# One of four channel blocks of the wide convolution moved to GpSimd

## What is computed

```
def conformer_conv(h_val, h_gate, dw_w, dw_b, ln_g, ln_b):
    h = h_val * jax.nn.sigmoid(h_gate)
    h = causal_depthwise_conv(h, dw_w) + dw_b        # 31 taps, 512 channels
    h = layer_norm(h, ln_g, ln_b)
    return jax.nn.silu(h)

def hybrid_mixer(x, w_in, ...):
    h = x @ w_in
    c_val, c_gate, q, k, v, z, b_logit, a_logit = jnp.split(h, IN_SPLITS_2, axis=-1)
    y_conv = conformer_conv(c_val, c_gate, ...)
    y_dn = gated_deltanet(q, k, v, z, b_logit, a_logit, ...)
    return jnp.concatenate([y_conv, y_dn], axis=-1) @ w_out
```

## Time and profile before

| | |
|---|---|
| median of the three runs | 2535.86 us |
| the profiled execution | 2543.58 us |
| its span | 2541.5 us |
| TensorE busy | 96% of the span |
| VectorE busy | 74% |
| ScalarE busy | 56% |
| GpSimd busy | 0.2 us |
| mixer A, from the first projection to the last output product | about 995 to 1177 us |
| mixer B | about 1375 to 1561 us |

### The profile page before, as it was taken

The page is one execution under the profiler, slowest core; times in us unless marked ns, Lnnn a source line. Parts: engine busy times, 40 slices in busy tenths (PEclk is TensorE's granted clock), DMA queues, the critical chain, the costliest instruction groups (busy, mean ns, idle before and its releaser), DMA issues.

```text
span 2541.5 us, 36256 instructions
## 1 busy us (share of the span) xinstructions
PE 2433.5 (96%) x14462; PEld 2103.4 (83%) x14462; DVE 1880.7 (74%) x2198; ACT 1424.2 (56%) x1578; POOL 0.2 (0%) x4
## 2 busy tenths in 40 slices
PE   7999999999999999989999998999999999999897
PEld 7999989899998998886997885787777777888786
DVE  7665755567657543986554985889999999988787
ACT  4654444456545343423342422678888888777574
POOL 0000000000000000000000000000000000000000
PEclk9999999999999999999999998999999999999998
DMA  6333464343345444304534302899999999999796
GB/s 253 138 119 133 154 244 183 149 146 145 117 162 203 178 188 165 134 36 166 199 150 155 145 3 100 337 360 404 412 412 413 413 413 412 382 347 367 287 354 261
DMA packets 119623, 593.19 MB, mean 233 GB/s; under 512 B 17440, under 2 KB 17824, under 8 KB 77472
## 3 DMA queue, kind: packets, MB, share of 16 engines
q1 hardware_dynamic: 110224, 585.40, 59.8%
q10 hardware_dynamic: 9232, 5.47, 0.8%
HBM read 589.79 MB, written 1.05 MB: 232 GB/s over the span
## 4 chain that ended last, share of the span: by engine, by line
PE 69%; DVE 18%; DMA 5%; issue 4%; ACT 3%; DVEq 0%; SPq 0%; ACTq 0%; POOLq 0%
PE bank L608 21%; PE bank L2512 17%; PE bank L865 12%; DVE wlo L687 6%; DMA ring<-in_stream 5%; PE bank L1717 4%; DVE ring_lo L839 2%; ACT whi L682 2%; PE bank L1133 2%; DVE big L2967 1%; PE bank L1148 1%; PE bank L1738 1%; PE bank L1903 1%; PE bank L2452 1%; DVE big L2141 1%
## 5 line engine op out<-in xcount | busy, mean ns | idle before, releaser
L687 DVE TENSOR_TENSOR wlo<-ring,whi 128x2048 fp32r<-128x2048 f32 x430 | 979.0, 2289 | 113.0 <-ACT whi L682 108.8
L682 ACT ACTIVATE whi<-ring 128x2048 fp32r<-128x2048 f32 x433 | 825.9, 1912 | 111.6 <-PE bank L2512 51.4
L2512 PE MATMUL bank<-whi,xhi 128*128 128x512 f32 x896 | 367.7, 410 | 16.3 <-DVE wlo L687 12.5
L2512 PE MATMUL bank<-wlo,xhi 128*128 128x512 f32 x896 | 353.0, 394 | 0.0
L839 DVE TENSOR_TENSOR ring_lo<-ring,slot_hi 128x1024 fp32r<-128x1024 f32 x160 | 192.5, 1222 | 136.2 <-ACT slot_hi L816 125.9
L608 PE MATMUL bank<-xhi,whi 128*128 128x256 f32 x864 | 244.5, 283 | 2.4 <-DVE xlo L570 1.3
L608 PE MATMUL bank<-xhi,wlo 128*128 128x256 f32 x864 | 244.5, 283 | 0.0
L608 PE MATMUL bank<-xlo,whi 128*128 128x256 f32 x864 | 244.5, 283 | 0.0
L816 ACT ACTIVATE slot_hi<-ring 128x1024 fp32r<-128x1024 f32 x160 | 166.5, 1052 | 109.1 <-PE bank L865 79.1
L2512 PEld LDWEIGHTS bank<-whi,xhi 128*128 128x128 f32 x896 | 170.0, 190 | 64.8 <-DVE wlo L687 31.5
L865 PE MATMUL bank<-xh,slot_hi 128*128 128x256 f32 x704 | 203.1, 288 | 3.0 <-DVE ring_lo L839 3.0
(11 more groups left out here) (525 smaller groups left out, 4508.7 us busy)
## 6 DMA issues: line engine op xcount, KB each, us to landing
ring<-in_stream SPq DMA_DIRECT2D x555, 1024.0 KB, 7.2
par<-in_par ACTq DMA_DIRECT2D x2, 2048.0 KB, 9.1
con<-in_con SPq DMA_DIRECT2D x1, 1216.0 KB, 10.8
X<-in_x SPq DMA_DIRECT2D x2, 512.0 KB, 4.1
out_y<-X SPq DMA_DIRECT2D x2, 512.0 KB, 2.6
par<-in_par ACTq DMA_DIRECT2D x2, 448.0 KB, 6.0
par<-in_par ACTq DMA_DIRECT2D x2, 157.5 KB, 3.3
con<-in_con SPq DMA_DIRECT2D x1, 64.0 KB, 4.3
```

The lines of the kernel that those rows point to most:

```text
L682: act.activation(whi[:, k % NSPLIT, :], src, ACT.Copy).then_inc(act_done, AC.step(tag + f".w{k}"))
L687: v.tensor_tensor(wlo[:, k % NSPLIT, :], src, whi[:, k % NSPLIT, :].bitcast(F32), ALU.subtract)\
L2512: mm = pe.matmul(out, left, right, start=start and i == 0, stop=stop and i == len(pairs) - 1)
```

## The change

GpSimd computes block 3 in each mixer. It waits for `gated1`, makes the first tap with the bias, and then for each of 30 taps one multiplication into a product tile, `scr[:, 1, 768:1024]`, and one addition into `ca`. A semaphore of its own, `pool_taps`, goes up with each of these 61 instructions, and each waits for the one before. VectorE's steps of pair 1 make block 2 alone. Three waits for the 61st are added: TensorE's before the sum over the channels, VectorE's before the copy of N2 (whose neighbour N2 + I takes the tile of the products) and VectorE's before the centring.

```diff
+        pool_taps = sem("pool_taps")
...
                 if lev == 1:
                     pe.wait_ge(vec_done, VE.at(tag + "cc"))
+                    pe.wait_ge(pool_taps, 2 * CONV_WIN - 1)
                     pe.wait_ge(vec_done, VE.at(tag + "vb"))
                     over_channels(PS[6], lambda b: ca[:, b, :], "cmu")
...
             for t in range(NT):
                 v.wait_ge(pe_done, PE.at(tag + f"N2{t}"))
+                v.wait_ge(pool_taps, 2 * CONV_WIN - 1)
                 v.tensor_copy(mN2[t], PS[3 * t + 2][:, :]).then_inc(vec_done, VE.step())
...
                 if lev == 1:
+                    v.wait_ge(pool_taps, 2 * CONV_WIN - 1)
                     v.wait_ge(pe_done, PE.at(tag + "cmu"))
...
             for w in range(first, last):
-                for b in (2 * pair, 2 * pair + 1):
+                for b in (0, 1, 2)[2 * pair:2 * pair + 2]:
                     tap = dw[:, b * CONV_WIN + w:b * CONV_WIN + w + 1]
...
         @block.gpsimd
         def _(pool):
+            def last_block(tag):
+                b, product = 3, scr[:, 1, 768:1024]
+                pool.wait_ge(vec_done, VE.at(tag + "gated1"))
+                for w in range(CONV_WIN):
+                    src, at = cv[:, b, w:w + T], b * CONV_WIN + w
+                    if w == 0:
+                        pool.tensor_scalar(ca[:, b, :], src, p2("dww")[:, at:at + 1], p2("dwb")[:, b:b + 1], ALU.mult,
+                                           ALU.add).then_inc(pool_taps, 1)
+                        continue
+                    pool.wait_ge(pool_taps, 2 * w - 1)
+                    pool.tensor_scalar(product, src, p2("dww")[:, at:at + 1], None, ALU.mult).then_inc(pool_taps, 1)
+                    pool.wait_ge(pool_taps, 2 * w)
+                    pool.tensor_tensor(ca[:, b, :], ca[:, b, :], product, ALU.add).then_inc(pool_taps, 1)
+
             def body(tag):
                 def f(it):
-
+                    if tag in ("mixA", "mixB"):
+                        last_block(tag[3:])
                     pool.wait_ge(arrived, it * 4 + 4 * (seg_no[tag] + 1))
                     pool.sem_inc(pool_turns, 1)
-                    for s in (pe_done, act_done, vec_done, slots_used, slots_split):
+                    for s in (pe_done, act_done, vec_done, slots_used, slots_split, pool_taps):
                         pool.sem_clear(s)
```

## The result

The changed kernel takes 2550.33 us (median of 7 runs) where the kernel before takes 2535.95 (7 runs): 14.4 us more, a ratio of 1.0052 with a 95% interval of 1.0042 to 1.0063. It is slower, as forecast, by 14.4 us where 30.5 were forecast. The traces are of one execution each, and that of the kernel before took 2543.58 us: most executions of that kernel lie at 2532 to 2538 us, some (on two of the chips about half) at 2539 to 2544. In a second measurement, on the chip of the last experiment, the ratio was 1.0056 (1.0041 to 1.0070).

A forecast was written before the change was run, and what follows sets the result against it. TensorE, 96% busy, was taken to bound the kernel, with VectorE's work counting only where TensorE waits for it. Contention gave +13.8 in A, +15.0 in B and +1.7 for the clock: +30.5 on 2535.86, so 2566.4 us, range 2526 to 2594.

The forecast's parts named there:

- Rival 1: GpSimd's work costs VectorE nothing in either mixer: gain 7.3 us, 2528.6 us; chance 0.28.
- rival 2: GpSimd's block ends late and stalls VectorE's copy of N2 in each mixer: +28 us, 2564; chance 0.07.
- Two of the signs: GpSimd's 61 instructions from 1028.4 end near 1078; TensorE idles over 10 us before its norm sums in both mixers.
- 25.0 lost: VectorE, second gating to norm sums: each GpSimd instruction takes its whole time from a two-operand instruction, 61 x 0.41 us a mixer.
- the stretch: Stretch (a), second gating's end to end of projection 7's short convolution, 34.5 us: all of the block's price falls there.
- Less the idle: VectorE's waits for ScalarE before the norm sums absorb lost time: 5.25 us in A, 3.61 in B.
- 1.1 saved: VectorE before the end of projection 7's short convolution: four of pair 1's steps become single, 1.1 us a mixer.
- the slack of 1.4: Mixer A, before the norm sums: ScalarE's square ends at 1064.34, TensorE takes it up at 1065.78, 1.44 us absorbed.
- Forecast: 17.2: Mixer A: TensorE's norm sums come 17.2 us later, after savings, idle and slack are taken off the 25.0.
- 18.9: Mixer B: 18.9 us later, as 25.0 less 1.1, 3.61 of idle and 1.44 of slack.
- The gains: Behind the norm sums, shorter TensorE waits from VectorE's earlier decay product and following steps: 3.4 us in A, 3.9 in B.
- the 1.7 that I took for both: TensorE's low clock after the long idle before the norm sums: 1.7 us taken of 3.2 for both mixers.

The follow-up runs named there:

- the last experiment: Kernel before with four of VectorE's steps made earlier and nothing on GpSimd: 2538.08 us, ratio 1.0000; the changed kernel was run again beside it.
- the block made twice: Changed kernel, but GpSimd's 61 instructions go into a tile nobody reads and VectorE makes all four blocks: 2575.12 us, 1.0144 of the kernel before.
- twelve taps: Changed kernel, but GpSimd makes only block 3's first 12 taps, VectorE the rest, with its steps regrouped: 2551.36 us, 1.0054 of the kernel before.
- two inputs: Changed kernel with GpSimd's 30 multiplications by a scalar replaced by multiplications of two tensors, giving other numbers: 2839 us, in brackets.
- Without the block: Changed kernel with only the first of GpSimd's 61 instructions, block 3's other 30 taps left out: 2533.18 us, 0.9987 of the kernel before.
- changed again: The changed kernel run once more, unaltered, on the chip of the run with another VectorE order: 2551.07 us, 1.0056 of the kernel before.
- order alone: Kernel before with four of VectorE's ten steps around the decay product made earlier, nothing on GpSimd: 2538.08 us, ratio 1.0000.
- half width: Changed kernel with GpSimd's 60 instructions behind the first on 128 columns in place of 256: 2536.00 us, 0.9993 of the kernel before.
- one-input: Changed kernel with GpSimd's 30 additions replaced by multiplications by a scalar, so all 61 read one tensor: 2538.51 us, 1.0007 of the kernel before.

## Why the prediction was right and wrong

**The sign and the mechanism were right, the size was not.** Rival 1 (no contention) is out by the taps of 0.94 and 0.69 us and by the block made twice; rival 2 (GpSimd late) by the 23 us between its end and the copy. The rule of the Trainium skill on the shared pair of ports ("SBUF — State Buffer", "Who interferes with whom") agrees in what it separates: a two-operand instruction is held by a GpSimd instruction that reads, and by none that only writes. By its rule that one engine has the pair "for the whole instruction" the cost would be up to 0.97 and 0.72 us here; 0.22 and 0.47 were measured, and the measurement decides. The addition that the prediction estimates at 0.56 us lasts 0.72. Two of the signs weren't met: GpSimd ends at 1084.22 and not near 1078, and TensorE idles 6.3 us ahead of the norm sums in both mixers and not over 10. The range's upper end holds a slip: half of 0.41 us again is 0.62 an instruction and gives 2591, not 2594.

**The term that was mis-sized is "25.0 lost".** It had 61 instructions at 0.41, each taking turns with one of VectorE's, all ahead of the norm sums. Each factor was off. An instruction takes 0.22 or 0.47 of VectorE, 0.345 as a mean. GpSimd's own are 0.97 and 0.75 us long and 0.94 apart, more than twice the row that I took, so VectorE runs three instructions for two of GpSimd's; taking turns one for one never came about. And so only 46 of the 61 (43 us by 0.94) fall into the stretch, and a part of these lies beside PSUM operands and idle, where they cost nothing: 13.2 us in place of 25.0. The rest falls beside the taps ahead of the reciprocal and the short convolution of projection 8, under TensorE's projections 9 and 10. I had priced GpSimd's pace only for the question of whether it is in time, not for where its price falls.

**"Less the idle" was wrong the other way**, and hides a part of the first error. I took in all of the idle (5.25 and 3.61 us). The changed kernel still idles 1.40, and the run with twelve taps the full 2.78. Mixer A: 13.2 held - 1.1 saved - 3.85 of idle taken in = 8.3, against 8.5 by which the short convolution of projection 7 ends later (43.1 and 34.6 us behind the gating's end); less the slack of 1.4 it is the 7.1 that TensorE shows. Forecast: 17.2. Mixer B: 8.7 for 18.9.

**The gains were about right, where they were counted.** From projection 9 to the first N2 product TensorE took 33.3 us in A and 33.7 in B; after the change 30.0 and 30.2: 3.3 and 3.5 us, for 3.4 and 3.9 forecast. The clock behind the norm sums cost 2.1 and 1.4 us, twice the 1.7 that I took for both. These terms make 7.1 + 8.7 - 3.3 - 3.5 + 3.5 = 12.5 us, against 14.4 by the medians. The spans of the two traces differ by 6.5 only, since parts that the change leaves alone vary as well: behind the first output product of mixer B all traces but that with two inputs take between 1007.2 and 1013.2 us, 1012.8 before and 1007.2 changed.

**What I had not in the sum** is the clock elsewhere, and how much it takes back is open. Without the block TensorE gains 3.5 and 4.0 us between projection 9 and N2, and the run is 2 to 3.3 us faster, not 7. A drop of some 3 us in the recurrence stands in A, in B, in both or in neither of the traces: before in B, changed in A, without the block in A, changed again in neither, order alone in both. The two traces of the changed kernel, from two series, differ in it at nearly the same time (2550.10 and 2550.82 us), so one trace doesn't say what a kernel's executions have. What brings the drop on was not tried, and that it takes back the gain is a guess.

## What to carry to other kernels

- Before work of VectorE goes to GpSimd beside it, count the reads of both: here a tap with two SBUF operands on VectorE cost 0.40 us there, and 0.69 us of VectorE when GpSimd made another (0.47 for the addition, 0.22 for the multiplication). Such an offload could have paid here only beside VectorE's idle, its instructions with a PSUM operand or the RECIPROCAL, which lost nothing; no run tried it there.
- Idle of an engine isn't slack until it is known what ends it. Where it ends with an answer to the engine's own earlier instruction, it moves along.
- Price the helper engine's pace as well as its toll: the pace says which stretch of the critical engine the toll lands in.

## What the runs showed of the hardware

- GpSimd, 128x256 float32: multiplication by a per-partition scalar 0.92 to 0.97 us, addition of two tensors 0.72 (0.84 where it met VectorE's lone, chained taps), memset 0.31, and 0.06 to 0.1 from the end of one to the start of its dependent. The one-input instruction is the longer of the two, at half width too (0.60 and 0.45 at the shortest), yet holds VectorE for less than half of the other's time.
- It is mostly VectorE that is held, but not always. At half width GpSimd's addition takes 0.67 us beside taps and 0.45 without them. Single multiplications take 1.24 us (changed kernel, 1474.50), 1.26 (half width, 1044.37) and 1.41 (one-input, 1041.97), and the taps beside them 0.47 to 0.62: there GpSimd is held. What decides it was not tried.
- VectorE is held early in GpSimd's instruction: a tap that begins 0.10 us into a multiplication takes 0.69 us, one that begins 0.72 into it 0.47, and line 2215, two SBUF operands of 4x512, begins 0.40 into one (1081.01) and takes its 0.68.
- Held were taps with two SBUF operands and the first tap with one (0.41 to 0.81). Eight instructions with one operand in PSUM took 2.16 us alone and beside GpSimd, and the RECIPROCAL 3.33 and 3.34.
- The clock's drop in the recurrence costs about 3 us of TensorE (41.2 us or 44.0 to 44.4) and changes its place between kernels whose TensorE work is the same, and between two executions of one.
